# Experts' idle products placed ahead of the ranks, late pieces asked for first, the last group's sums reordered, and attention's samples four abreast

## The chip, the cores and the metric

One core of one Trainium2 chip runs the whole program in one launch. The metric is the time of one execution on the device in microseconds (us); a kernel's figure is the median of its runs.

## The reference

One step of a two-layer decoder in float32, for 256 prompt tokens and 8 samples of 4 new tokens (288 rows of 1024 in all).

```python
h = x + gdn_mixer(rms_norm(x))                    # layer 0: gated DeltaNet
h = h + hier_moe(rms_norm(h), layer 0)            # 32 experts, top 1 group, top 2 in it
k, v = shared_kv(h)                               # rotary keys
h = h + diff_mixer(rms_norm(h), k, v)             # layer 1: differential attention, 8 heads
h = h + hier_moe(rms_norm(h), layer 1)
y = rms_norm(h)

# an expert, d_ff 512:  (silu(x @ w_gate[e]) * (x @ w_up[e])) @ w_down[e]
# differential attention, head of 2 x 64: softmax of each half, a = p[0] - lam * p[1], o = a @ v
# samples attend to 256 cached keys (two pages of 128, from a page table) and their own 4
```

The outputs are the normed rows, the new keys and values, and the DeltaNet and convolution states.

## The kernel before

The program is a sequence of phases with a barrier of all engines after each: `gdn_phase`, `moe_phase` of layer 0, `attn_phase`, `moe_phase` of layer 1, `final_phase`. Each phase gives every engine its own list of work, and semaphores order them. Every float32 product or transpose is two instructions on TensorE.

**Expert layer (`moe_phase`).** The 32 experts are taken two by two in 16 groups (`LAST` is 15). An expert takes up to 64 rows; a pair fills 128 partitions. Weights come in pieces of 2 MB, one matrix of one expert each, six to a group in the order gate, gate, up, up, down, down. They go into ten slots by number (`p % 10`). SP asks for a piece when the products that read its slot have been made (`used`). Pieces 0 to 9 fit in at the start: some are asked for in the phase ahead; in layer 0 4, 5, 7 and 8, in layer 1 4 and 5, at the start of this phase, after the stores of the normed rows (`xn_dram`, which POOL's gathers read); piece 9 only when the stores have landed and group 0's rows have been made. Pieces 10 and 11 wait for group 0's gate products.

The front: TensorE transposes the rows and makes the router's logits; VectorE works out the two experts of each row (`both`, L2105, semaphore `hots`); TensorE counts ranks (L2311 to L2316); VectorE makes a selection matrix for group 0 (`sel0`, L2118); TensorE makes group 0's rows with it (L2411) and the tables for POOL's gathers (L2417), and then the group's gate, up and down products. `keep_busy(n)` issues n products whose result nobody reads (L2306); they keep TensorE at work while it waits. There are 20 ahead of the ranks and 8 behind.

A group in the middle (`gate_up`, `rows_T`, `products`): gate stage (L2334), the transposes of the last group's selection (`sel_T`, L2365), up stage (L2334), the five sums of the group before (`combine`, L2372 and L2375: four of 128x512 and one of the 32 sample rows) with the transposes of the hidden rows between (`hid_T`, L2342), the next group's rows (L2325), the down stage (L2348). A stage is 32 instructions. VectorE adds each sum to the residual rows (`add`, L2222; L2226 for the four parts of the sample rows), forms the hidden product (`hidden`, L2191) and the selection (`selection`). In the last group the sums of group 14 come after the up stage, as elsewhere, and its own five after the down stage, the sample rows' last.

**Attention samples (`attn_phase`, `samples(pair)`).** The 8 samples go in 4 pairs. For a pair TensorE transposes the keys of 2 samples x 2 pages x 8 heads (L1650), VectorE and ACT copy them to `XK`; it makes the scores (L1659), where `QBs` holds the queries of each head in a 64-column block that is zero elsewhere, so that the 8 heads add up into 64 rows a sample, two samples abreast; 12 idle products (L1637) run while VectorE and ACT make the softmax; it combines and transposes the weights (L1664 to L1666), makes the values (L1677) in four 32-column strips, one head each, and transposes the result (L1684), from which VectorE copies each head's own rows (L1520). SP asks for the next pair's keys when a pair's transposes are made and for its values when the value products are; ahead of pair 1's keys it asks for `w_out` (4 MB) and one piece for layer 1.

## Time and profile before

| | |
|---|---|
| median of 3 runs | 1651.73 us (1651.51 to 1653.41) |
| the profiled execution | 1656.28 us, span 1654.5 us |
| mean granted TensorE clock | 0.969 of full speed |
| TensorE busy, its weight loads, VectorE, ScalarE, POOL | 93%, 49%, 40%, 16%, 5% of the span |
| transfers | 485.55 MB, 293 GB/s over the span |
| expert layers, from their first product to their last sum | 365.8 to 857.3 us and 1152.2 to 1641.0 us |
| attention | 858.3 to 1151 us, its sample pairs 969.7 to 1053.6 us |

The span runs from the first to the last instruction; the execution's own time is longer by what lies around it. Busy shares are averages over phases with different limits, and a waiting engine is only of interest where its work is what the phase ends with. "Granted clock" is the share of TensorE's 2.4 GHz that the chip let through.

### The profile page before, as it was taken

The page shows a single profiled execution, that of the slowest core. Times are in us where ns is not written, and L with a number is a line of the kernel's source. Part 1 is how long each engine was busy: PE and PEld are TensorE (multiplying, and loading weights), DVE is VectorE, ACT ScalarE, POOL GpSimd, SP SyncE. Part 2 cuts the span into 40 slices and gives each one's busy share as a digit, 9 for nine tenths or more (in the row PEclk, how much of TensorE's full clock was granted, in tenths as well). Part 3 has the DMA queues.
Part 4 walks back from the last instruction along what each step waited for, and adds up shares of the span by engine and source line. Part 5 has one row for each costly group of instructions (what it writes and reads, how often), then busy time and mean ns, then how long its engine had stood idle before and what let it go on. Part 6 is the DMA issues. An engine that isn't in the chain of part 4 may idle for free. (4 is left out here: it accounts for less than half of the span.)

```text
span 1654.5 us, 21283 instructions
## 1 busy us (share of the span) xinstructions
PE 1541.2 (93%) x8183; PEld 802.8 (49%) x8183; DVE 658.3 (40%) x1654; ACT 268.1 (16%) x653; POOL 82.1 (5%) x139
## 2 busy tenths in 40 slices
PE   9999998998999999989989978869999999998995
PEld 8787776666333333333334445654633333333332
DVE  2756475445324232423252232552532433242424
ACT  2424334220000000000020011451000000000001
POOL 0101010100000000000000000100000000000000
PEclk9999999998999999999989989989899999999998
DMA  6432413438999999999991265603699999999993
GB/s 215 137 107 70 134 43 128 183 131 325 429 429 430 430 430 430 431 431 430 423 352 39 102 258 207 219 5 148 229 429 431 430 430 429 430 431 430 431 420 122
DMA packets 95052, 485.55 MB, mean 293 GB/s; under 512 B 15338, under 2 KB 50062, under 8 KB 70914
## 3 DMA queue, kind: packets, MB, share of 16 engines
q1 hardware_dynamic: 90658, 480.08, 71.6%
q0 software_dynamic: 4320, 4.42, 0.8%
q8 instruction: 54, 0.88, 0.2%
q14 instruction: 20, 0.16, 0.0%
HBM read 484.82 MB, written 10.97 MB: 300 GB/s over the span
## 5 line engine op out<-in xcount | busy, mean ns | idle before, releaser
L2334 PE MATMUL moe_ps_up<-slots,moe_xrT 128*64 128x512 f32 x1024 | 234.8, 612 | 26.4 <-DMA slots<-in_w_up_e_dram 26.4
L2334 PE MATMUL moe_ps_gate<-slots,moe_xrT 128*64 128x512 f32 x1024 | 229.0, 600 | 0.0
L2348 PE MATMUL moe_ps_y<-slots,router_inputs 128*64 128x512 f32 x1024 | 226.8, 595 | 0.0
L2191 DVE TENSOR_TENSOR router_inputs<-router_inputs,moe_ps_up 128x512 f32<-128x512 f32 x32 | 22.0, 688 | 445.4 <-PE moe_ps_up L2334 445.4
L2334 PEld LDWEIGHTS moe_ps_up<-slots,moe_xrT 128*64 128x64 f32 x1024 | 78.5, 141 | 158.2 <-issue 157.5
L2334 PEld LDWEIGHTS moe_ps_gate<-slots,moe_xrT 128*64 128x64 f32 x1024 | 76.1, 138 | 146.9 <-issue 146.8
L2348 PEld LDWEIGHTS moe_ps_y<-slots,router_inputs 128*64 128x64 f32 x1024 | 70.5, 137 | 133.2 <-issue 132.7
L907 PE MATMUL gdn_bank<-gdn_xT,slots 128*128 128x288 f32 x512 | 133.0, 409 | 0.7 <-ACT slots L455 0.7
L907 PEld LDWEIGHTS gdn_bank<-gdn_xT,slots 128*128 128x128 f32 x512 | 93.9, 190 | 24.8 <-issue 1.8
L2012 ACT COPY moe_xrT<-moe_ps_x 128x512 f32<-128x512 f32 x32 | 18.8, 586 | 423.4 <-PE moe_ps_x L2325 393.5
L2372 PE MATMUL moe_ps_x<-moe_y_sb,router_inputs 128*128 128x512 f32 x128 | 63.8, 618 | 0.0
L2214 DVE COPY moe_y_sb<-moe_ps_y 128x512 f32<-128x512 f32 x30 | 20.8, 692 | 91.8 <-PE moe_ps_y L2348 91.8
L1981 POOL DMA_INDIRECT moe_xrT<-xn_rows,moe_rows_in x30 | 30.9, 1030 | 478.6 <-PE moe_ps_x L2325 476.7
L2226 DVE TENSOR_TENSOR resid<-resid,moe_ps_up 32x256 f32<-32x256 f32 x128 | 52.9, 413 | 3.0
L2222 DVE TENSOR_TENSOR resid<-resid,moe_ps_x 128x512 f32<-128x512 f32 x64 | 44.0, 688 | 23.9 <-PE moe_ps_x L2372 23.9
L2017 ACT ACTIVATE router_inputs<-moe_ps_gate 128x512 f32<-128x512 f32 x32 | 19.1, 598 | 206.8 <-PE moe_ps_gate L2334 206.8
L2206 DVE TENSOR_SCALAR moe_place<-consts,moe_lpos,moe_gcur 128x128 f32<-128x128 f32 x192 | 52.1, 345 | 1.2
L2027 ACT COPY moe_y_sb<-moe_ps_y 128x512 f32<-128x512 f32 x32 | 18.8, 586 | 206.5 <-PE moe_ps_y L2348 206.5
L1613 PE MATMUL at_bank<-slots,at_XK 128*128 128x512 f32 x96 | 44.1, 622 | 0.0
L2372 PEld LDWEIGHTS moe_ps_x<-moe_y_sb,router_inputs 128*128 128x128 f32 x128 | 21.7, 189 | 41.3 <-issue 41.3
L1613 PE MATMUL at_pair<-slots,at_XK 128*128 128x512 f32 x96 | 41.5, 592 | 0.0
L665 DVE SCALAR_TENSOR_TENSOR slots<-slots,gdn_cw 128x312 f32<-128x312 f32 x72 | 39.2, 545 | 2.5
(486 smaller groups left out, 1925.8 us busy)
## 6 DMA issues: line engine op xcount, KB each, us to landing
slots<-in_w_gate_e_dram SPq DMA_DIRECT2D x64, 2048.0 KB, 31.2
slots<-in_w_up_e_dram SPq DMA_DIRECT2D x64, 2048.0 KB, 29.7
slots<-in_w_down_e_dram SPq DMA_DIRECT2D x60, 2048.0 KB, 31.3
slots<-in_w_in_a_dram SPq DMA_DIRECT2D x16, 1024.0 KB, 5.6
slots<-in_w_down_e_dram SPq DMA_DIRECT2D x8, 1024.0 KB, 29.8
slots<-in_w_kv_dram SPq DMA_DIRECT2D x4, 2048.0 KB, 17.3
slots<-in_cache_k_dram SPq DMA_DIRECT2D x16, 512.0 KB, 5.0
slots<-in_cache_v_dram SPq DMA_DIRECT2D x16, 512.0 KB, 5.5
```

The costliest lines, as they stand in the source:

```text
L665: ins = V.scalar_tensor_tensor(acc[:, a, j, 0:ACC_COLS], src, cw[:, a, j, tap:tap + 1], acc[:, a, j, 0:ACC_COLS], ALU.mult, ALU.add)
L907: last = T.matmul(PB[i % 2][:, 0:T_ALL], w4[:, j, k, 128 * a:128 * a + 128], xT[:, k, :], start=(k == 0), stop=(k == KT - 1))
L1613: last = T.matmul(bank[:, :], XK[:, 0 if j < 2 else 1, k, at[t]], wslot[3 * half + j][:, k, :], start=(k == 0), stop=(k == KT - 1))
L1981: pool.indirect_dma_start(xg, None, xn_dram[:, :], bass.IndirectOffsetOnAxis(rows_in[:, :], 0), bounds_check=T_ALL - 1, oob_is_err=False). ...
L2191: V.tensor_tensor(hid, hid, ps_up[:], ALU.mult).then_inc(s["hidden"], 1)
L2206: last = V.tensor_scalar(place[:, k, t, :], m["lanes"][:, :], where[:, k, t:t + 1], gcur[:, k, t:t + 1], ALU.is_equal, ALU.mult)
L2214: V.tensor_copy(y_sb[:, 0:512], ps_y[:, 0]).then_inc(s["y0_kept"], 1)
L2222: V.tensor_tensor(half, half, banks[i][:, :], ALU.add).then_inc(s["summed"], 1)
L2226: V.tensor_tensor(part, part, banks[i][32 * q:32 * q + 32, 0:256], ALU.add).then_inc(s["summed"], 1)
L2334: last = T.matmul(ps[64 * e:64 * e + 64, :], xgT[:, k, 64 * e:64 * e + 64], slots[:, slot[2 * n + e], 512 * k:512 * k + 512], start=(k == ...
L2348: last = T.matmul(ps_y[64 * e:64 * e + 64, h, :], hidT[:, k, 64 * e:64 * e + 64], slots[:, slot[4 + e], 1024 * k + 512 * h:1024 * k + 512 ...
L2372: last = T.matmul(banks[i][:, :], selT[:, at[t]], y_sb[:, 512 * h:512 * h + 512], start=True, stop=True)
```

## The change

- The 28 idle products of the expert layer's front: 38 ahead of the ranks, none behind them.
- SP asks for the late pieces at the start of the expert phase, ahead of the rows' stores.
- Last group: group 14's sums come after the gate stage and the selection's transposes, ahead of the up stage; the fifth of them goes to `ps_y`'s first bank. Then up, `sel_T(LAST)`, `hid_T(LAST)`, down. The last group's own sums are six: the two of the left half, the sample rows' two left parts, their two right parts, the two of the right half.
- Attention samples: scores of four heads a strip (two strips a sample, four abreast), the queries in blocks of 32 columns; value products of 512 columns (four heads' values at once) in four strips, 24 instructions a pair for 96; four copies of the result a pair for two. The constants follow the new order of the rows.

In the diff, edits of constants and counts that follow from these are left out.

```diff
-        QBs = sb("QBs", [128, 2, H, 64])
+        QBs = sb("QBs", [128, 2, H, 32])
...
-        QB = flat[1][:, 0:4096].rearrange("p (b h r) -> p b h r", b=DEC_BATCH, h=H)
+        QB = flat[1][:, 0:2048].rearrange("p (b h r) -> p b h r", b=DEC_BATCH, h=H)
...
             for c in range(2):
                 for h in range(H):
-                    V.tensor_copy(QB[64 * c:64 * c + 64, :, h, 32 * c + 4 * h:32 * c + 4 * h + 4],
+                    V.tensor_copy(QB[64 * c:64 * c + 64, :, h, 16 * c + 4 * (h % 4):16 * c + 4 * (h % 4) + 4],
                                   qTd[64 * c:64 * c + 64, h, :].rearrange("p (b q) -> p b q", q=DEC_SEQ)).then_inc(s["QB_made"], 1)
...
                 for b in range(2):
-                    own = (B[3][:, 0:36 * H], B[3][:, 512 - 36 * H:])[b].rearrange("p (h r) -> p h r", h=H)[:, :, (0, 32)[b]:(0, 32)[b] + DEC_SEQ]
-                    V.tensor_copy(oT[:, :, bass.ds(8 * pair + (SEQ + DEC_SEQ * b), DEC_SEQ)], own).then_inc(s["od_kept"], 1)
+                    for f in range(2):
+
+                        base, lo = 64 * b + 48 * f + 12, 16 * (b * f)
+                        own = B[3][:, lo:lo + 496].rearrange("p (j r) -> p j r", j=4)[:, :, base - lo:base - lo + DEC_SEQ]
+                        V.tensor_copy(oT[:, 4 * f:4 * f + 4, bass.ds(8 * pair + (SEQ + DEC_SEQ * b), DEC_SEQ)], own).then_inc(s["od_kept"], 1)
...
-                for h in range(H):
+                for h in range(4):
                     for b in range(2):
-                        last = T.matmul(B[0][64 * b:64 * b + 64, 0:T_ALL], QBs[:, b, h, :], XK[:, b, h, :], start=(h == 0), stop=(h == H - 1))
+                        for f in range(2):
+                            lane = 64 * b + 32 * f
+                            last = T.matmul(B[0][lane:lane + 32, 0:T_ALL], QBs[:, b, 4 * f + h, :], XK[:, b, 4 * f + h, :],
+                                            start=(h == 0), stop=(h == 3), tile_position=(0, lane))
                 last.then_inc(s["S_made"], 1)
 
                 keep_busy(B[1], 256, 12)
@@ -1667,19 +1675,17 @@
                 pe.wait_ge(s["aT_kept"], 2 * pair + 2)
                 pe.wait_ge(s["V0_in"], 64 * pair + 64)
 
-                for b in range(2):
-                    for f in range(2):
-                        for i in range(N_PAGES + 1):
-                            for h in range(4 * f, 4 * f + 4):
-                                values = Vc[:, b, i, 128 * h:128 * h + 128] if i < N_PAGES else v_t[0:T_DEC, 2, 128 * h:128 * h + 128]
-                                weights = aT[:, i, 32 * b:32 * b + 32] if i < N_PAGES else aT[0:T_DEC, 2, 32 * b:32 * b + 32]
-                                lane = 32 * (h % 4)
-                                last = T.matmul(B[2][lane:lane + 32, 256 * b + 128 * f:256 * b + 128 * f + 128], weights, values,
-                                                start=(i == 0), stop=(i == N_PAGES), tile_position=(0, lane))
+                for i in range(N_PAGES + 1):
+                    for b in range(2):
+                        for f in range(2):
+                            lane, e = 64 * b + 32 * f, slice(512 * f, 512 * f + 512)
+                            values = Vc[:, b, i, e] if i < N_PAGES else v_t[0:T_DEC, 2, e]
+                            weights = aT[:, i, 32 * b:32 * b + 32] if i < N_PAGES else aT[0:T_DEC, 2, 32 * b:32 * b + 32]
+                            last = T.matmul(B[2][lane:lane + 32, :], weights, values, start=(i == 0), stop=(i == N_PAGES), tile_position=(0, lane))
                 last.then_inc(s["od_made"], 1)
                 pe.wait_ge(s["rows_kept"], pair + 1)
                 if later(pair):
-                    pe.wait_ge(s["od_kept"], 2 * pair)
+                    pe.wait_ge(s["od_kept"], 4 * pair)
                 for j in range(4):
                     last = T.transpose(B[3][:, 128 * j:128 * j + 128], rot[:, 128 * j:128 * j + 128], ident[:, :])
                 last.then_inc(s["od_T"], 1)
...
         ps_sum = [flat_x[0], flat_x[1], ps_tab, ps_gate, ps_up]
-        ps_sum_last = [flat_x[1], ps_tab, ps_gate, flat_x[0], ps_up]
+        ps_sum_14 = [flat_x[0], flat_x[1], ps_tab, ps_gate, ps_y[:, 0, :]]
+        ps_sum_last = [flat_x[1], ps_tab, ps_gate, flat_hid, flat_x[0], ps_up]
+        LAST_SUMS = [(0, 0), (0, 1), (0, 2), (1, 2), (1, 0), (1, 1)]
...
         @block.sync
         def _(sp):
+            m["prefetch"](sp, layer, (4, 5) if layer else (4, 5, 7, 8))
             for t in range(NT):
                 sp.wait_ge(s["normed"], t + 1)
                 sp.dma_start(xn_dram[128 * t:128 * t + rows[t], :], xn[0:rows[t], t, :]).then_inc(s["xn_stored"], 16)
-            m["prefetch"](sp, layer, (4, 5))
             if layer == 0:
-                m["prefetch"](sp, layer, (7, 8))
                 m["attn_inputs"](sp)
             sp.wait_ge(s["xn_stored"], 16 * NT)
...
+            for i in range(5):
+                add(LAST - 1, i, ps_sum_14)
             selection(LAST, False, lpos, gcol[:, :, :, LAST])
             hidden(LAST)
-            for i in range(3):
-                add(LAST - 1, i, ps_sum)
             turned(LAST)
-            for i in range(3, 5):
-                add(LAST - 1, i, ps_sum)
             dve.wait_ge(s["y_h0"], 1)
             V.tensor_copy(y_sb[:, 0:512], ps_y[:, 0]).then_inc(s["y0_kept"], 1)
-            for i in range(5):
-                add(LAST, i, ps_sum_last)
+            for i in range(6):
+                dve.wait_ge(s["sum_made"], 5 * LAST + i + 1)
+                h, t = LAST_SUMS[i]
+                if t < 2:
+                    half = resid[:, t, 512 * h:512 * h + 512]
+                    V.tensor_tensor(half, half, ps_sum_last[i][:, :], ALU.add).then_inc(s["summed"], 1)
+                else:
+                    for q in range(2 * h, 2 * h + 2):
+                        part = resid[0:T_DEC, 2, 256 * q:256 * q + 256]
+                        V.tensor_tensor(part, part, ps_sum_last[i][32 * q:32 * q + 32, 0:256], ALU.add).then_inc(s["summed"], 1)
...
 
             pe.wait_ge(s["xT_kept"], 2 * NT)
-            keep_busy(20)
+            keep_busy(38)
...
                 T.matmul(ps_count, ones[0:rows[t], :], both[0:rows[t], t, :], start=(t == 0), stop=(t == NT - 1))
-            keep_busy(8)
             xgv = by_tile(xg)
...
             slot, filled = pieces(LAST)
-            gate_up(LAST, slot, filled)
+            pe.wait_ge(s["gx_kept"], 2 * LAST + 2)
+            pe.wait_ge(s["silued"], LAST)
+            pe.wait_ge(s["summed"], 8 * LAST - 12)
+            stage(0, ps_gate, slot, filled)
+            sel_T(LAST - 1, flat_hid)
+            outputs_kept(LAST - 1)
+            for i in range(5):
+                if i == 3:
+                    pe.wait_ge(s["silued"], LAST + 1)
+                combine(LAST - 1, i, ps_sum_14)
+            pe.wait_ge(s["hidden"], LAST)
+            pe.wait_ge(s["summed"], 8 * LAST - 8)
+            stage(1, ps_up, slot, filled)
+            pe.wait_ge(s["summed"], 8 * LAST)
             sel_T(LAST, flat_x[0])
+            hid_T(LAST)
             pe.wait_ge(s["hid_kept"], MAIN_GROUPS)
             for h in range(2):
                 pe.wait_ge(down_half[h], 32)
                 down(slot, h).then_inc((s["y_h0"], s["y_made"])[h], 1)
-            pe.wait_ge(s["summed"], 8 * LAST)
             pe.wait_ge(s["sel_kept"], MAIN_GROUPS)
-            for i in range(5):
-                if i in (0, 2):
-                    pe.wait_ge((s["y0_kept"], s["y1_kept"])[i // 2], MAIN_GROUPS)
-                combine(LAST, i, ps_sum_last)
+            for i in range(6):
+                h, t = LAST_SUMS[i]
+                if i in (0, 3):
+                    pe.wait_ge((s["y0_kept"], s["y1_kept"])[h], MAIN_GROUPS)
+                if t < 2:
+                    last = T.matmul(ps_sum_last[i][:, :], selT[:, at[t]], y_sb[:, 512 * h:512 * h + 512], start=True, stop=True)
+                else:
+                    for q in range(2 * h, 2 * h + 2):
+                        last = T.matmul(ps_sum_last[i][32 * q:32 * q + 32, 0:256], selT[:, at[2]], y_sb[:, 256 * q:256 * q + 256], start=True, stop=True,
+                                        tile_position=(0, 32 * q))
+                last.then_inc(s["sum_made"], 1)
```

## Rows read from the trace of the kernel before

**Rows 1.** Waits inside the expert layers: engine and line waited for whom, us, times, longest.
```profile
PE moe_ps_up L2334 <- DMA slots<-in_w_up_e_dram: 26.4, 14, 2.5
```
**Rows 2.** Windows: length, busy PE, PEld, DVE, ACT, POOL, clock, DMA share, GB/s.
```profile
404.00:408.00 4.00, 4.00 (x22) 1.42 (x20) 3.60 (x23) 0.00 (x0) 0.00 (x0) 1.00 0.45 181
...
412.00:416.00 4.00, 4.00 (x22) 1.60 (x18) 0.59 (x1) 0.00 (x0) 0.00 (x0) 1.00 0.99 426
```
**Rows 3.** Timeline, layer 0's front: start, length, engine, line; in brackets idle time before.
```profile
373.66 4.73 PE L2306 MATMUL moe_ps_gate<-consts 128*128 128x128 f32 x40
...
382.37 0.26 DVE L2105 TENSOR_TENSOR moe_both<-moe_oneh 128x96 f32<-128x96 f32 x1
...
382.68 0.46 PE L2311 MATMUL moe_ps_up<-moe_both,consts 128*128 128x96 f32 x2 [4.29 <-DVE moe_both L2105]
...
384.55 1.07 DVE L2118 TENSOR_SCALAR moe_y_sb<-moe_y_sb,moe_pos 128x64 f32<-128x64 f32 x6
...
385.65 3.78 PE L2306 MATMUL moe_ps_gate<-consts 128*128 128x128 f32 x16
...
389.23 8.71 PE L2411 MATMUL moe_ps_x<-moe_y_sb,moe_last_slot 128*128 128x128 f32 x48
...
399.66 8.78 PE L2334 MATMUL moe_ps_gate<-slots,moe_xrT 128*64 128x512 f32 x32
```
**Rows 4.** Windows of the same front; the third number from the end is the granted clock.
```profile
384.00:386.00 2.00, 2.00 (x9) 1.87 (x9) 1.58 (x9) 0.00 (x0) 0.00 (x0) 0.50 1.05 451
...
400.00:402.00 2.00, 2.00 (x8) 0.61 (x6) 1.76 (x10) 0.00 (x0) 0.89 (x2) 0.52 0.92 307
```
**Rows 5.** Timeline, layer 1's front.
```profile
1160.05 4.73 PE L2306 MATMUL moe_ps_gate<-consts 128*128 128x128 f32 x40
...
1167.50 0.26 DVE L2105 TENSOR_TENSOR moe_both<-moe_oneh 128x96 f32<-128x96 f32 x1
...
1174.43 8.65 PE L2411 MATMUL moe_ps_x<-moe_y_sb,moe_last_slot 128*128 128x128 f32 x48
```
**Rows 6.** Timeline, SP's queue in layer 0's front.
```profile
373.17 4.32 SPq L1904 DMA_DIRECT2D xn_rows<-moe_last_slot  x3
```
**Rows 7.** Timeline, layer 0's last group on TensorE.
```profile
827.72 0.61 PE L2365 MATMUL moe_ps_hid<-consts,moe_place 128*128 128x128 f32 x3
...
830.34 1.97 PE L2334 MATMUL moe_ps_up<-slots,moe_xrT 128*64 128x512 f32 x4 [2.00 <-DMA slots<-in_w_up_e_dram]
...
838.95 1.98 PE L2372 MATMUL moe_ps_x<-moe_y_sb,router_inputs 128*128 128x512 f32 x4
...
844.16 7.09 PE L2348 MATMUL moe_ps_y<-slots,router_inputs 128*64 128x512 f32 x32
```
**Rows 8.** Timeline, layer 1's last group.
```profile
1612.99 0.61 PE L2365 MATMUL moe_ps_hid<-consts,moe_place 128*128 128x128 f32 x3
...
1627.84 6.66 PE L2348 MATMUL moe_ps_y<-slots,router_inputs 128*64 128x512 f32 x30
...
1639.20 1.75 DVE L2226 TENSOR_TENSOR resid<-resid,moe_ps_up 32x256 f32<-32x256 f32 x4
```
**Rows 9.** Timeline, the scores and the values of pair 3.
```profile
1039.40 4.10 PE L1659 MATMUL at_pair<-at_XK,at_QBs 128*64 128x288 f32 x32 [0.75 <-ACT at_XK L1367]
...
1047.90 0.64 PE L1677 MATMUL at_pair<-slots,at_aT 128*32 128x128 f32 x16 [0.50 <-DVE at_aT L1513]
...
1051.73 0.69 DVE L1515 COPY at_rot<-at_pair 128x512 f32<-128x512 f32 x1 [3.89 <-PE at_pair L1677]
```
**Rows 10.** Timeline: three strips abreast with their loads; transposes of pairs 1 and 3.
```profile
955.06 7.07 PE L1621 MATMUL at_pair<-slots,at_XK 128*32 128x512 f32 x48
...
955.51 0.12 PEld L1621 LDWEIGHTS at_pair<-slots,at_XK 128*32 128x32 f32 x3 [0.31 <-issue]
...
994.67 3.29 PE L1650 MATMUL at_bank<-consts,slots 128*128 128x128 f32 x16 [4.38 <-DMA slots<-in_cache_k_dram]
...
1034.05 1.96 PE L1650 MATMUL at_bank<-consts,slots 128*128 128x128 f32 x16
```

More of the change, by code:

```diff
@@ L1176, in attn_constants @@
     c["causal"] = np.concatenate([causal, np.zeros((128, 128)), causal], 1)
-    rb, rc, rh, rq = p // 64, (p // 32) % 2, (p // 4) % 8, p % 4
+    rb, rc, rq = p // 64, (p // 16) % 2, p % 4
+    rh = 4 * ((p // 32) % 2) + (p // 4) % 4
     kb, kq = np.arange(T_DEC) // DEC_SEQ, np.arange(T_DEC) % DEC_SEQ
@@ L1183, in attn_constants @@
     col = np.arange(64)
-    c["halves"] = (rb[:, None] == col // 32) & (rh[:, None] == (col // 4) % 8) & (rq[:, None] == col % 4)
+    ch = 4 * ((col // 16) % 2) + 3 - (col // 4) % 4
+    c["halves"] = (rb[:, None] == col // 32) & (rh[:, None] == ch) & (rq[:, None] == col % 4)
     c["first_half"] = rc[:, None] == 0
@@ L1528, in _ @@
             st["base"], st["n"] = PAIRS * S_STEPS + pre, 0
-            dve.wait_ge(s["od_kept"], 2 * PAIRS)
+            dve.wait_ge(s["od_kept"], 4 * PAIRS)
             V.tensor_tensor(rot2[:, 0:256].rearrange("p (h r) -> p h r", h=H), oT[:, :, SEQ:], oT[:, :, SEQ:], ALU.mult).then_inc(s["od_sq"], 1)
@@ L2214, in kept, with add @@
                 V.tensor_copy(y_sb[:, 0:512], ps_y[:, 0]).then_inc(s["y0_kept"], 1)
-            def add(g, i, banks):
-                dve.wait_ge(s["sum_made"], g * 5 + i + 1)
+            def add(g, i, banks, extra_sum=0):
+                dve.wait_ge(s["sum_made"], g * 5 + (i + 1 + extra_sum))
                 if i < 4:
@@ L2272, in _ @@
                     for i in range(5):
-                        add(g, i, ps_sum)
+                        add(g, i, ps_sum, 1)
                 dve.wait_ge(s["summed"], extra * 8 + 8 * MAIN_GROUPS)
```

## The prediction

> **What bounds the kernel now.** I first read where the expert layers wait, since they fill most of the span. In the list of waits TensorE's one large wait inside them is for the up-projection pieces, some 1.9 us at a time [rows 1]. In the windows the transfers stand nearly still in the last microseconds before group 0's gate products end, and afterwards run at 426 GB/s [rows 2]. The reader should see two regimes: until gate(0) has ended nothing more can be asked for (the slots are full), and from then on the weight stream never stops until the last group's up piece lands. So an expert layer's end is *end of gate(0)* + *a stream of fixed bytes* + *the tail after the last up piece*. TensorE work in the middle is worth nothing; a microsecond before the end of gate(0), or in the tail, is worth a microsecond. Then I read the timeline of the fronts [rows 3, 5] with the granted clock [rows 4], the SP queue [rows 6], the tails [rows 7, 8] and the sample pairs of attention [rows 9], which are a chain without an overlap from pair to pair.
>
> **Front, idle products.** Now 20 idle products (40 instructions) take 4.73 us to 378.4, TensorE then idles to 382.68, and the clock is 0.50 while it does the ranks and the 8 idle products behind them [rows 3, 4]. Those 8 run from 385.65, and the rows' products (L2411) start only at 389.23, although their input, the selection of L2118, is ready at 384.55 + 1.07 = 385.62.
> With 38 in front: 76 instructions x 0.114 us (4.73 less a tail of 0.17, by 40) = 8.7 us, so TensorE is free at 373.66 + 8.7 = 382.3, before L2105 ends at 382.63. Layer 0 loses nothing by it. In layer 1 the free time is 1160.05 + 8.7 = 1168.75 against 1167.76 [rows 5]: 1.0 late. The ranks' eight instructions at half clock take 382.68 to 384.35; I take 1.1 us at full clock (0.6 less). L2118 then ends at about 385.1 (layer 0) and 1171.2 (layer 1), and the counts' six instructions are done before. L2411 starts at 385.2 instead of 389.23, **4.0 us** earlier, and at 1171.25 instead of 1174.43, **3.2 us** earlier.
> What removing the 8 may cost: they are what TensorE does just before the clock comes back. Without them 2.7 us of tiny products and waiting stand before L2411, and a low spell in it is likely, as one follows the idle stretch now, and another the small products ahead of gate(0) [rows 4]. Gate(0) lost 8.78 - 7.09 = 1.7 us to such a spell [rows 3, 7]: the row of the down products shows what 32 such instructions take at the full clock. L2411 loses less, since at full clock it already takes 8.7/48 = 0.18 us per instruction against 0.114 for the idle ones: between 0 and 1.7, I take **1.0 us per layer**. The spell in gate(0) itself I leave as it is; if it goes, 1.7 per layer come on top. Fronts: 3.0 + 2.2 = **5.2 us**. Bounds: 2.6 for the two together (spells at 1.7 each and the ranks no faster) and 7.2 + 3.4 = 10.6 (no spell at all).
>
> **Late pieces ahead of the rows.** SP now holds the rows' stores at 373.17 to 377.5 ahead of the late pieces [rows 6]; the change asks for pieces 4, 5, 7, 8 at about 366 in layer 0. Moved past are three stores of rows, and behind the pieces in layer 0 the five attention inputs, not due for 500 us. 4 x 2.1 MB at 426 GB/s [rows 2] is 19.7 us: the pieces are in by 388 and the stores (1.15 MB) by 391. The stores are late next, and two things wait for them: piece 9 on SP, which must also wait for L2411's end (385.2 + 8.7 + 1.0 = 394.9), and the gather of POOL, which waits for the table, 2 us later still. Both are later than 391: cost nothing, cover 4 us. The gain is a condition, not a term: L2411 ending early would otherwise find the four pieces still in transfer, and piece 9 and the pieces asked for at gate(0)'s end behind them; now the queue is empty by then. In layer 1 two pieces move over an idle queue: nothing.
>
> **Last group.** TensorE now waits 2.00 us for the up piece, then makes up(15), and only then sums group 14 [rows 7]. The change sums group 14 (4.2 us of products: 838.95 to 844.16 less 0.5 each for the hidden product's and the selection's transposes) ahead of up(15).
> Layer 0: gate(15) ends 827.72, transposes 0.6, ACT's copy of the selection until 828.8, sums until 833.05. Up(15) 7.1 us, to 840.1; hidden product 0.7, its transposes 0.5, their copy 0.7, three handovers: down starts at 842.3 instead of 844.16, **1.9 us**. Most of this is that up(15) began after 2 us of idling and took 838.95 - 830.34 = 8.6 us instead of 7.1; that idling goes.
> Layer 1: gate(15) ends 1612.99 [rows 8], so by the same steps sums until 1618.3, up(15) to 1625.4, down at 1627.6 instead of 1627.84, **0.2 us**. The sums that left the way behind up(15) are paid nearly in full by its later start.
> Last sums: VectorE is the limit, four additions of 0.69 and four small ones of 1.75 together, 4.5 us; now it waits a little for each product and has the four small ones last [rows 8]. With small ones in the middle it should wait for nothing after the first: about 0.35 us per layer, **0.7 us**. Tails: **2.8 us**; bounds 0.5 and 4.
>
> **Attention samples.** Scores: 32 instructions two abreast in 4.10 us [rows 9], that is 16 steps of 0.24 and the last one's tail. The same 32, four abreast, are 8 steps: 8 x 0.24 + 0.17 = 2.1, **2.0 less**. That four column strips share a step at full rate is read from three: L1621's 48 instructions of 512 columns take 7.07 us [rows 10], 16 steps of 0.43 (and 0.24/288 per column is the same rate).
> Values: 96 instructions of 128 columns from 1047.90 to about 1051.67, 3.77 us [rows 9]; now 24 of 512. The columns are the same: 24 x 0.107 before and 6 x 0.43 after, both 2.56. Gained is the overhead at the seven changes between full and 32-row operands, of which one stays: 3.77 - (2.56 + 0.13 + 0.17) = **0.9 less**. The Trainium skill (TensorEngine Tiling, Tiling Modes) says that changing the tiling mode drains TensorE; the row agrees.
> Per pair 2.9 us. But pair 1 begins when its keys land: TensorE idles 4.38 us and more before 994.67 [rows 10], and the keys are asked for when pair 0's have been transposed, which the change doesn't move. Pair 0's 2.9 us go into that wait. What pair 1 gains after its keys stays, and the later pairs' transposes wait for no transfer [rows 10]: 3 x 2.9 = 8.7 us. The four small copies of the outputs instead of two cost VectorE 0.3 us each pair, hidden by the next pair's transposes save in the last: 8.7 - 0.3 = **8.4 us**. POOL's copies and clearing halve, off the path. Bounds: 4 (below) and 9.
>
> **Sum.** 5.2 + 2.8 + 8.4 = 16.4 us. The profiled execution took 1656.28 us (span 1654.5); it gives 1639.9. The median of the runs lies 4.55 below that execution, so 1651.73 - 16.4 = **1635.3 us**.
>
> **Rivals.**
> *No low spells in the fronts.* The early, gapless idle products keep the clock through gate(0). For it: the spell now follows an idle stretch that is filled. Against it: the second spell follows small products that stay. 16.4 + 2.0 + 3.4 = 21.8: 1629.9 us.
> *Loads don't hide.* Four strips of the same rows: if a step had to wait for its loads, 0.12 us for the group [rows 10], the scores would take 8 x 0.36 + 0.17 = 3.05 and the values 6 x 0.55 + 0.3 = 3.6, per pair 1.2 less instead of 2.9, and the sum is 11.3: 1640.4 us. L1621's steps show no such addition with three strips. The Trainium skill (TensorE: Matmul & The Clock Gate, Part 3: Packing small matmuls) states this rule, that weight loads overlap running products only where the row groups differ; the trace speaks against it.
> *The fronts give nothing.* TensorE at half clock from the ranks through L2411 eats the 4.0 and 3.2, or the stores come so late that piece 9 holds up the stream: 11.2 left, 1640.5 us.
> *Slower.* One mechanism: with fewer instructions under way the clock falls in the sample pairs. Price: pair 1's first 16 transposes took 3.29 us at the low clock [rows 10]; the same 16 in pair 3, at the full clock, took 1.96. Applied to all TensorE work of a pair (about 11 us of 16) it is some +11 per pair, +34 for three, and the total +17: 1669 us. It decides from half of the pairs' time on. Against it: the change halves one stretch of 4.1 us, and the 12 idle products stay.
> *It does nothing*: the stream would have to be set by something other than gate(0)'s end, and attention by transfers.
>
> **How the numbers follow.** Forecast 0.62, no spells 0.18, loads 0.06, fronts nothing 0.09, slower 0.03, nothing 0.02. The range goes from the no-spells case with a little of the bounds, 1628, to the two weaker ones, 1641.5. What can be told from no change is about 0.2%, 3.3 us: all cases but the last two are faster by more. Faster 0.95, same 0.02, slower 0.03.
>
> **What would show it.** After: no idling between idle products and ranks; L2411 about 2.6 us (layer 0) and 3.5 us (layer 1) behind L2105's end instead of 6.6 and 6.7; the score products about 2.1 us per pair, the value products 2.9; the wait for pair 1's keys longer by 2.9; up(15) in both layers starting without a wait for its piece and some 2.7 us after it lands; last VectorE additions of 512 columns. The stream must still be unbroken from gate(0) on. It would be wrong if the clock is at 0.50 through all of L2411 and gate(0), if the scores take over 3 us, or if the rows' stores land after L2411 ends.

## The result, and the profile after

| | before | after |
|---|---|---|
| median of 12 runs | 1657.64 us (1651.51 to 1660.91) | 1645.63 us (1641.24 to 1649.47) |
| the profiled execution | 1656.28 us, span 1654.5 us | 1645.96 us, span 1644.2 us |
| mean granted TensorE clock | 0.969 | 0.968 |

The ratio of after to before is **0.9932, 95% interval [0.9916, 0.9948]**: faster by 11.3 us (8.6 to 13.9) where the sum said 16.4. Two things stand between 1635.3 and 1645.63, and they are kept apart below. The median of before rose from 1651.73 to 1657.64 us with nine more runs: 5.9 us of the miss is the base that the sum was taken from. The other 4.4 us (5.1 by the ratio) are terms of the sum.

I cut both spans at the same events. In us, before and then after:

| stretch | before | after | change | forecast |
|---|---|---|---|---|
| start to layer 0's experts | 365.8 | 366.5 | +0.7 | |
| layer 0: front, to the start of up(0) | 42.5 | 45.6 | **+3.1** | -3.0 |
| layer 0: up(0) to the end of gate(15) | 419.5 | 419.4 | 0 | 0 |
| layer 0: tail, to attention's first product | 30.6 | 28.5 | -2.1 | -2.2 |
| attention | 293.9 | 282.5 | -11.3 | -8.4 |
| of it the four sample pairs | 84.4 | 76.4 | -8.0 | -8.4 |
| layer 1: front | 41.3 | 37.6 | -3.6 | -2.2 |
| layer 1: up(0) to the end of gate(15) | 419.6 | 422.7 | +3.2 | 0 |
| layer 1: tail, to the last sum | 28.0 | 27.5 | -0.5 | -0.55 |
| final phase | 13.6 | 13.8 | +0.3 | |

The rows sum to -10.3, the difference of the spans, 6.1 us short of the forecast. Layer 0's front is 6.1 off and layer 1's expert stream 3.2; the first and the last row add 1.0; attention (2.9) and layer 1's front (1.4) came out better than forecast. So one front went the wrong way, and it weighs as much as the whole miss. Timeline of layer 0's front after the change:

```profile
374.38 8.75 PE L2319 MATMUL moe_ps_gate<-consts 128*128 128x128 f32 x76
...
383.07 0.26 DVE L2112 TENSOR_TENSOR moe_both<-moe_oneh 128x96 f32<-128x96 f32 x1
...
383.38 0.46 PE L2324 MATMUL moe_ps_up<-moe_both,consts 128*128 128x96 f32 x2 [0.25 <-DVE moe_both L2112]
...
384.70 1.07 DVE L2125 TENSOR_SCALAR moe_y_sb<-moe_y_sb,moe_pos 128x64 f32<-128x64 f32 x6
...
385.82 14.25 PE L2423 MATMUL moe_ps_x<-moe_y_sb,moe_last_slot 128*128 128x128 f32 x48 [0.58 <-DVE moe_y_sb L2125]
400.00 3.18 PE L2429 MATMUL moe_ps_tab<-moe_entry,moe_place 128*128 128x32 f32 x12
...
403.11 9.15 PE L2346 MATMUL moe_ps_gate<-slots,moe_xrT 128*64 128x512 f32 x32
```

Up to 385.82 it goes as forecast: the idle products fill the wait, the ranks start 0.3 us behind L2112 (the old L2105), and the selection is ready at 385.77. Then the same 48 instructions that took 8.71 us [rows 3] take 14.25. Windows of that stretch (the third number from the end is the granted clock, the next the DMA share):

```profile
384.00:386.00 2.00, 1.42 (x12) 1.27 (x12) 1.77 (x12) 0.00 (x0) 0.00 (x0) 1.00 1.01 426
386.00:388.00 2.00, 2.00 (x10) 1.56 (x10) 1.90 (x8) 0.00 (x0) 0.00 (x0) 0.70 1.07 295
388.00:390.00 2.00, 2.00 (x8) 1.52 (x7) 1.44 (x10) 0.00 (x0) 0.00 (x0) 0.50 0.79 242
...
396.00:398.00 2.00, 2.00 (x8) 1.45 (x7) 0.00 (x0) 0.00 (x0) 0.00 (x0) 0.50 0.00 0
...
404.00:406.00 2.00, 2.00 (x8) 0.71 (x6) 1.78 (x8) 0.00 (x0) 1.20 (x1) 0.50 0.97 418
406.00:408.00 2.00, 2.00 (x8) 0.52 (x6) 1.73 (x10) 0.00 (x0) 0.00 (x0) 0.68 0.60 232
408.00:410.00 2.00, 2.00 (x12) 0.62 (x10) 1.97 (x14) 0.00 (x0) 0.27 (x1) 1.00 0.03 8
```

The clock is full through the ranks, at its lower level (0.50) from about 387 to 407.3, and full again from 408: one low spell of 20 us, where before there were two shorter ones [rows 4] with the rows' products at full clock between them. TensorE is busy all the while. Before, the clock was back just as the rows' products had begun behind the eight idle ones, as these windows of that kernel show:

```profile
388.00:390.00 2.00, 2.00 (x11) 1.95 (x10) 1.28 (x9) 0.00 (x0) 0.00 (x0) 0.54 0.98 418
390.00:392.00 2.00, 2.00 (x14) 1.57 (x12) 0.00 (x0) 0.00 (x0) 0.00 (x0) 1.00 0.99 426
```

After the change the DMA share is near nothing from 394 on, so the late pieces and the rows' stores have landed, 3 us later than estimated and still 6 before L2423 ends. Layer 1's front, with the same code, has no such spell; its timeline:

```profile
1150.39 8.75 PE L2319 MATMUL moe_ps_gate<-consts 128*128 128x128 f32 x76
1158.97 0.36 PE L2324 MATMUL moe_ps_up<-moe_both,consts 128*128 128x96 f32 x2
...
1161.31 8.51 PE L2423 MATMUL moe_ps_x<-moe_y_sb,moe_last_slot 128*128 128x128 f32 x48 [0.58 <-DVE moe_y_sb L2125]
1171.54 8.78 PE L2346 MATMUL moe_ps_gate<-slots,moe_xrT 128*64 128x512 f32 x32
```

and the window of its rows' products, with the clock at 1.00:

```profile
1161.00:1170.00 9.00, 8.69 (x51) 6.76 (x51) 3.86 (x21) 0.14 (x1) 0.00 (x0) 1.00 0.01 2
```

Attention's samples, timeline of TensorE from pair 1's keys to pair 2's, against [rows 9, 10]:

```profile
994.96 3.32 PE L1655 MATMUL at_bank<-consts,slots 128*128 128x128 f32 x16 [6.97 <-DMA slots<-in_cache_k_dram]
...
1001.68 2.15 PE L1666 MATMUL at_pair<-at_XK,at_QBs 128*32 128x288 f32 x32 [0.75 <-ACT at_XK L1369]
...
1008.25 1.92 PE L1684 MATMUL at_pair<-slots,at_aT 128*32 128x512 f32 x16 [0.50 <-DVE at_aT L1515]
1010.10 1.06 PE L1684 MATMUL at_pair<-at_v,at_aT 32*32 32x512 f32 x8
...
1012.66 1.96 PE L1655 MATMUL at_bank<-consts,slots 128*128 128x128 f32 x16
```

The scores are the 2.1 us of the forecast, the values 2.91 (1008.25 to 1011.16) against 2.9. The wait for pair 1's keys grew from 4.38 to 6.97 us: pair 0's gain went in there.

Layer 0's last group, and the end of layer 1's sums on VectorE, against [rows 7, 8]:

```profile
832.67 1.96 PE L2384 MATMUL moe_ps_x<-moe_y_sb,router_inputs 128*128 128x512 f32 x4 [0.58 <-ACT router_inputs L2029]
...
836.84 7.09 PE L2346 MATMUL moe_ps_up<-slots,moe_xrT 128*64 128x512 f32 x32
...
844.72 0.74 PE L2354 MATMUL moe_ps_hid<-consts,router_inputs 128*128 128x128 f32 x4 [0.24 <-DVE router_inputs L2198]
846.25 7.09 PE L2360 MATMUL moe_ps_y<-slots,router_inputs 128*64 128x512 f32 x32 [0.78 <-DVE router_inputs L2203]
```

```profile
1627.30 0.84 DVE L2273 TENSOR_TENSOR resid<-resid,moe_ps_gate 32x256 f32<-32x256 f32 x2
1628.18 0.87 DVE L2273 TENSOR_TENSOR resid<-resid,moe_ps_hid 32x256 f32<-32x256 f32 x2
1629.08 0.69 DVE L2269 TENSOR_TENSOR resid<-resid,moe_ps_x 128x512 f32<-128x512 f32 x1
1629.68 0.68 DVE L2269 TENSOR_TENSOR resid<-resid,moe_ps_up 128x512 f32<-128x512 f32 x1
```

Up(15) follows the sums without a wait, and the additions run without gaps.

### The profile page after: what moved, and what is told of

The parts are those of the page before. It is cut to its first block and busy times, and to the rows that moved or that the text cites. A ratio compares the mean times of both kernels' runs of the same rounds, so it can differ in the third digit from the quotient of the medians.

```text
span 1644.2 us, 20799 instructions
## 1 busy us (share of the span) xinstructions
PE 1535.7 (93%) x7935; PEld 793.2 (48%) x7935; DVE 658.9 (40%) x1662; ACT 268.1 (16%) x653; POOL 79.1 (5%) x139
## 5 line engine op out<-in xcount | busy, mean ns | idle before, releaser
L2346 PEld LDWEIGHTS moe_ps_gate<-slots,moe_xrT 128*64 128x64 f32 x1024 | 76.2, 139 | 149.0 <-issue 148.9
L2384 PE MATMUL moe_ps_x<-moe_y_sb,router_inputs 128*128 128x512 f32 x120 | 59.5, 618 | 1.2 <-ACT router_inputs L2029 1.2
L2229 DVE TENSOR_TENSOR resid<-resid,moe_ps_x 128x512 f32<-128x512 f32 x60 | 41.3, 688 | 32.0 <-PE moe_ps_x L2384 32.0
L2233 DVE TENSOR_TENSOR resid<-resid,moe_ps_up 32x256 f32<-32x256 f32 x112 | 46.3, 413 | 2.6
```

What stands on the lines that cost most here:

```text
L2229: V.tensor_tensor(half, half, banks[i][:, :], ALU.add).then_inc(s["summed"], 1)
L2233: V.tensor_tensor(part, part, banks[i][32 * q:32 * q + 32, 0:256], ALU.add).then_inc(s["summed"], 1)
L2346: last = T.matmul(ps[64 * e:64 * e + 64, :], xgT[:, k, 64 * e:64 * e + 64], slots[:, slot[2 * n + e], 512 * k:512 * k + 512], start=(k == ...
L2384: last = T.matmul(banks[i][:, :], selT[:, at[t]], y_sb[:, 512 * h:512 * h + 512], start=True, stop=True)
```

## The experiments

### One part alone

Three kernels: before with attention's edits, with the fronts' (idle products, late pieces), with the tails'.

> The kernel before with the attention samples four abreast and nothing else of the change. By the terms measured in the changed kernel's trace (scores 2.15 us a pair for 4.10, values 2.96 for 3.84, pairs 16.3 us apart for 19.0) pairs 1 to 3 give 8.1 us; the forecast said 8.4. If the profiled difference of the whole attention phase (294 us to 282.5, 11.3 us) is due to the edit, it is 11 us. If the rest of it is only where TensorE's low clock spells fell, about 8 us in the median. Fronts and tails as before: the rows' products (L2411 of before) start 6.6 us behind the end of the VectorE line that makes both.

> The kernel before with 38 idle products ahead of the ranks, none behind, and the late pieces asked for ahead of the rows' stores; attention and tails as before. Theory A (clock): without the idle products behind the ranks the clock can fall in front of the rows' products and, since these are thin, does not come back until the gate stage: in a layer where it falls they take about 14 us instead of 8.6 and the front ends 3 to 4 us later than before, in a layer where it doesn't the front is 3.5 us shorter. The median lies between -7 and +7 us, near 0, and the executions spread over 7 us. Theory B (transfers): the front is slow because the pieces of 2 MB and the rows' stores are now in transfer under the rows' products; then both layers, or always layer 0, show it, whatever the clock. My forecast of before said -5.2 us.

> The kernel before with only the last group's order changed. Forecast 2.8 us less (2.2 in layer 0, 0.6 in layer 1), which the changed kernel's trace bears out for layer 0 (2.1). If a low clock spell in up(15) of layer 0 was most of that gain and falls elsewhere in other executions, about 1 us.

| | median us | ratio [interval] | in us of 1656 | forecast |
|---|---|---|---|---|
| attention only | 1646.65 | 0.9939 [0.9917, 0.9961] | -10.1 | -8.4 |
| fronts only | 1655.34 | 0.9985 [0.9968, 1.0001] | -2.5 | -5.2 |
| tails only | 1655.33 | 0.9993 [0.9977, 1.0009] | -1.2 | -2.8 |

Attention carries nearly the whole change; its interval, 6.5 to 13.6 us, takes in both the 8 and the 11 us of the expectation. That of the fronts takes in nothing and, at its edge, the forecast 5.2. With the fronts alone the spell is there too, so neither the tails nor attention make it. Its timeline, the rows' products of layers 0 and 1:

```profile
385.94 14.25 PE L2409 MATMUL moe_ps_x<-moe_y_sb,moe_last_slot 128*128 128x128 f32 x48 [0.58 <-DVE moe_y_sb L2117]
...
1178.94 8.51 PE L2409 MATMUL moe_ps_x<-moe_y_sb,moe_last_slot 128*128 128x128 f32 x48 [0.58 <-DVE moe_y_sb L2117]
```

The tails' interval takes in both nothing and the 2.8 us; the profile has to decide there, and shows up(15) and the sums as in the whole change.

### Is it the clock or the transfers?

Two theories for layer 0's front: the clock falls since nothing dense stands between the ranks and the rows' products, or the stores and pieces asked for together hold something up. First, the changed kernel with eight idle products back behind the counts:

```diff
                 T.matmul(ps_count, ones[0:rows[t], :], both[0:rows[t], t, :], start=(t == 0), stop=(t == NT - 1))
+            keep_busy(8)
```

> The changed kernel with the 8 idle products put back behind the ranks (38 in front, 8 behind). Theory A: the clock stays up through the rows' products in both layers, which take 8.6 us each; they start later by what the 8 cost at full clock beyond the wait for the selection, 16 x 0.114 = 1.8 less the 0.6 of waiting now there = 1.2 us. Layer 0's front ends 4 us earlier than in the changed kernel's profile, layer 1's 1.2 us later; the median of the kernel is lower than the changed kernel's by 0 to 3 us and its runs lie closer together. Theory B (transfers): the rows' products in layer 0 take 14 us again and everything is 1.2 us later in both layers.

1639.61 us, ratio 0.9892 [0.9869, 0.9915]. Its timeline, layer 0:

```profile
385.66 2.05 PE L2319 MATMUL moe_ps_gate<-consts 128*128 128x128 f32 x16
387.55 8.41 PE L2424 MATMUL moe_ps_x<-moe_y_sb,moe_last_slot 128*128 128x128 f32 x48
...
397.80 8.60 PE L2347 MATMUL moe_ps_gate<-slots,moe_xrT 128*64 128x512 f32 x32
```

Windows of it, with the clock at 1.00 where the changed kernel had 0.70 and 0.50:

```profile
386.00:388.00 2.00, 2.00 (x20) 1.96 (x18) 1.86 (x9) 0.00 (x0) 0.00 (x0) 1.00 1.09 344
388.00:390.00 2.00, 2.00 (x14) 1.55 (x12) 1.86 (x12) 0.00 (x0) 0.00 (x0) 1.00 0.88 211
```

Counted from the ranks, the eight delay the rows' products by 1.2 us; they shorten them by 5.8. Layer 0's front takes 39.3 us instead of 45.6. Layer 1's, where there was no spell to take away, takes 40.3 instead of 37.6: the 1.2 us of delay, and 1.5 us more in the table's products and gate(0) (2.54 and 9.64 us instead of 1.86 and 8.78). The profiles' fronts thus give 3.6 us together; the ratios differ by 6.6 us, with some 4.6 of uncertainty, where the expectation had 0 to 3. Then the other side, the changed kernel with the late pieces asked for behind the rows' stores, as before:

```diff
-            m["prefetch"](sp, layer, (4, 5) if layer else (4, 5, 7, 8))
             for t in range(NT):
...
+            m["prefetch"](sp, layer, (4, 5))
             if layer == 0:
+                m["prefetch"](sp, layer, (7, 8))
```

> The changed kernel with the late pieces asked for after the rows' stores, as before. Theory B (transfers under the rows' products slow them, or the stores behind the pieces hold something up): layer 0's rows' products are back at about 8.6 us. Theory A: they take 14 us as in the changed kernel, and as they end so late (400 us) the pieces are in either way: the ratio to the kernel before is that of the changed kernel, 0.993.

1646.38 us, 0.9934 [0.9908, 0.9960], against 0.9932 of the changed kernel, and the rows' products of layer 0 take 14.45 us. The order of the requests is not the cause, and it is worth nothing where the rows' products end as late as here; whether it is where they end early, at 392, no run shows. In another form, five idle products in the counts' place and the counts behind the rows' products:

```diff
-            for t in range(NT):
-                T.matmul(ps_count, ones[0:rows[t], :], both[0:rows[t], t, :], start=(t == 0), stop=(t == NT - 1))
+            keep_busy(5)
...
             last.then_inc(s["gx_T"], 1)
+            for t in range(NT):
+                T.matmul(ps_count, ones[0:rows[t], :], both[0:rows[t], t, :], start=(t == 0), stop=(t == NT - 1))
```

> The changed kernel, but the counts' six thin instructions come behind the rows' products and 5 idle products (10 instructions, 1.14 us) stand in their place, where TensorE waits for the selection. If it is the thin stretch between the ranks and the rows' products that lets the clock fall (theory A), the clock stays up in layer 0 as well, with no delay to the rows' products: 8.5 us in both layers and 5.5 us less than the changed kernel in the profile of layer 0. If a stretch as short as the four rank products and what is left of the wait still lets it fall, layer 0 shows about 14 us again. Layer 1 the same as in the changed kernel but for 0.9 us of counts, which come before the tables.

1641.38 us, 0.9907 [0.9884, 0.9930]; rows' products 8.51 us in both layers, and again layer 1's front is 2.5 us longer than the changed kernel's. The theory of the transfers fell, that of the clock stands: the two kernels that put idle products right ahead of layer 0's rows' products make them in 8.4 to 8.5 us. The four with the same order of the products and no idle ones right ahead (the changed kernel, the fronts alone, the one with the requests as before, and the one with late output weights further down) take 14.25, 14.25, 14.45 and 13.33, wherever the requests stand. By the windows the clock falls in these four only about 0.8 to 2.2 us after the rows' products have begun. What makes it fall is therefore not shown, only that either idle products ahead or another order of the products themselves (the next experiment) keeps the long spell away. Why layer 1, where the same work went by at full clock each time, is spared is open: what differs in the rows is that its ranks follow the idle products at once, while layer 0's wait 0.25 us for L2112, and no run here separates the two.

### Rows' products that are dense themselves

The loop goes tile by tile within a column block: 128 rows, 128 rows, 32 rows, eight times. Here the full-height tiles of all blocks come first and the 32-row tile's products last:

```diff
-            for k in range(KT):
-                for t in range(NT):
-                    last = T.matmul(ps_x[:, k // 4, k % 4, :], by_tile(xn[0:rows[t], t, :])[:, k, :], sel0[0:rows[t], t, :],
-                                    start=(t == 0), stop=(t == NT - 1))
+            for part in ((0, 1), (2,)):
+                for k in range(KT):
+                    for t in part:
+                        last = T.matmul(ps_x[:, k // 4, k % 4, :], by_tile(xn[0:rows[t], t, :])[:, k, :], sel0[0:rows[t], t, :],
+                                        start=(t == 0 and k % 4 == 0), stop=(t == NT - 1 and k % 4 == 3))
```

> The changed kernel with the rows' products of group 0 in another order: the 32 products of the two full tiles first, the 16 instructions of the 32-row tile after them, in place of a change between 128 and 32 rows at every sixth instruction. If the thinness of these products comes from those changes, as I read 0.178 us an instruction against 0.114 for the idle ones, they take 48 x 0.11 + 0.3 = 5.6 us instead of 8.5 at the full clock. Theory A (clock): they are then dense enough to bring the clock back where it has fallen: layer 0 no longer shows 14.25 us but 7 to 8, with one short low spell, and the low stretch that ran on into the gate stage is gone. Fronts 6 to 9 us (layer 0) and 3 us (layer 1) shorter than in the changed kernel's profile. Theory B (transfers): no more than 3 us in each. Against the kernel before: ratio 0.985 by A, 0.990 by B.

**1634.19 us, 0.9863 [0.9834, 0.9891].** Its timeline, both fronts:

```profile
386.06 5.82 PE L2424 MATMUL moe_ps_x<-moe_y_sb,moe_last_slot 128*128 128x128 f32 x48 [0.58 <-DVE moe_y_sb L2125]
393.59 8.79 PE L2346 MATMUL moe_ps_gate<-slots,moe_xrT 128*64 128x512 f32 x32
402.21 7.04 PE L2346 MATMUL moe_ps_up<-slots,moe_xrT 128*64 128x512 f32 x32
...
1154.96 5.82 PE L2424 MATMUL moe_ps_x<-moe_y_sb,moe_last_slot 128*128 128x128 f32 x48 [0.58 <-DVE moe_y_sb L2125]
```

The same instructions but for their order and their start flags: 14.25 to 5.82 us in layer 0 and 8.51 to 5.82 in layer 1. In layer 1 the clock was full in both, so the 2.7 us come from the order: of fifteen changes between 128-row and 32-row operands one is left, an estimate of 0.19 us for each of the fourteen. The Trainium skill (TensorEngine Tiling (Array Packing), Tiling Modes) says that a change of the tiling mode drains TensorE; the trace agrees as far as the changes cost time, but shows no drain as such. The rest of layer 0's gain, 5.7 us, is the clock.

With the idle products in the counts' place too:

> Both of the last two edits: fronts at the full clock with rows' products of 5.6 us. By theory A about 3 us a layer under the kernel with 8 idle products behind the ranks (which measured a ratio of 0.989), and no wait of 1.2 us for them: ratio 0.984 to 0.987. By theory B no better than that kernel.

1635.43 us, 0.9871 [0.9847, 0.9895]; 5.82 us in both layers, up(0) at 403.74. By the ratio no different from the tiles' order alone; in the profiles each front is some 2.5 us longer (38.0 and 37.3 us for 35.5 and 34.9), as the counts stand behind the rows' products and the tables and gate(0) run longer at the lower clock.

Then the order in the kernel before, where the eight idle products still stand (the edit is the same):

> The kernel before with nothing but the new order in the rows' products (tiles 0 and 1 of all column blocks first, the 32-row tile's products behind them). Theory (two separate costs): with the 8 idle products in place the clock is full there already, so what the order saves is only the changes between 128-row and 32-row operands, 8.7 to 5.8 us, 2.9 us in each layer; both end the stretch ahead of gate(0), so the total falls by 5.8 us, ratio 0.9965. Rival: the order helps only by bringing the clock back, which the kernel before doesn't need: then the rows' products stay at 8.5 us or the gain goes into the next wait, and the ratio is 1.000.

**This expectation missed.** 1655.06 us, ratio 1.0001 [0.9986, 1.0017]: nothing, where I had 5.8 us. The products did get shorter, by 2.3 and 2.9 us:

```profile
390.12 6.41 PE L2412 MATMUL moe_ps_x<-moe_y_sb,moe_last_slot 128*128 128x128 f32 x48
...
398.26 8.78 PE L2334 MATMUL moe_ps_gate<-slots,moe_xrT 128*64 128x512 f32 x32
...
1166.58 5.71 PE L2412 MATMUL moe_ps_x<-moe_y_sb,moe_last_slot 128*128 128x128 f32 x48
...
1174.59 9.79 PE L2334 MATMUL moe_ps_gate<-slots,moe_xrT 128*64 128x512 f32 x32
```

In layer 0 the front is 2.7 us shorter than before (39.8 us for 42.5), in layer 1 it is not (41.0 for 41.2): the clock was at 0.50 over that layer's start, its idle products take 5.87 us instead of 4.73, and gate(0) 9.79 instead of 8.78. The window of that start:

```profile
1142.00:1160.00 18.00, 16.74 (x87) 16.01 (x88) 12.30 (x27) 4.81 (x8) 1.62 (x2) 0.53 0.37 134
```

The profile of before has no such spell there. It is one execution, at 1648.87 us the shortest of the twelve, so it doesn't explain the median. To see all runs I took span x (1 - clock) of each, half the time at the lower clock, and means over the runs:

| kernel (runs) | mean span | clock | span x (1 - clock) |
|---|---|---|---|
| before, runs beside this one (17) | 1653.8 | 0.9671 | 54.4 us |
| before, full tiles first (12) | 1653.1 | 0.9654 | 57.2 us |
| changed (12) | 1643.6 | 0.9691 | 50.8 us |
| changed, full tiles first (6) | 1632.4 | 0.9723 | 45.2 us |

Read as what the clock cost, the order saves 3.5 us at full clock on the kernel before and loses 2.8 more to the clock; on the changed kernel it saves on both counts. This is a rough estimate. The 2.8 us have a standard error of some 1.6, and the split counts low time in which TensorE only waits as well. For the tails alone the same working gives 3.8 us more at full clock and 5.0 less to the clock, of an edit that hardly changes TensorE's work. Why the shorter products don't show in the time of the kernel before stays open.

### What delayed pair 1's keys

SP asks for `w_out` and one piece, 6.3 MB, ahead of them, and neither is needed before the end of attention. Moved behind pair 3's values:

```diff
-            sp.dma_start(w_out, m["w_out_b"][0].rearrange("(h p) n -> p h n", p=128)).then_inc(s["wout_in"], 16)
-            m["prefetch"](sp, 1, (3,))
             with sp.Fori(1, PAIRS) as pair:
                 cache(0, pair, True)
                 cache(1, pair, True)
+            sp.dma_start(w_out, m["w_out_b"][0].rearrange("(h p) n -> p h n", p=128)).then_inc(s["wout_in"], 16)
+            m["prefetch"](sp, 1, (3,))
```

> The changed kernel with one move on SP's queue: the output weights w_out (4.2 MB) and layer 1's piece 3 (2.1 MB), asked for ahead of pair 1's keys, are asked for behind pair 3's values. Theory (my account of the attention part): what pair 0 gained from the narrower products went into the wait for pair 1's keys, and that wait exists only because 6.3 MB are in front of the keys; then pair 1's transposes start as pair 2's do, as soon as pair 0's result is transposed, at 988 instead of 994.96 us: 7.0 us, and up to 1.4 us more as the 16 transposes behind the wait take 1.96 instead of 3.32 us at the full clock. The total falls by 7 to 8.4 us against the changed kernel. Rival: the keys are late for another reason (they are asked for only when pair 0's are transposed, and their own 2.1 MB take that long), or the wait moves on to pair 1's values; then the time stays within 2 us of the changed kernel's. The fronts aren't touched: the rows' products of layer 0 take 14.2 us as in the changed kernel.

> Both amendments together: the rows' products with the full-height tiles first, and w_out with piece 3 behind pair 3's values. They touch different phases, so both theories expect the sum: the 10 us that the order of the tiles gave, and 7 to 8.4 us where the output weights were what delayed pair 1's keys (a time near 1627 us, ratio to the kernel before near 0.981), or nothing more than the first where they weren't (near 1635 us, 0.986).

The first: 1635.70 us, 0.9869 [0.9851, 0.9887]; 10.4 us (0.63 points) below the changed kernel's ratio, with some 4 us of uncertainty, where 7 to 8.4 were expected. Its timeline, pairs 1 and 2:

```profile
987.09 1.91 PE L1655 MATMUL at_bank<-consts,slots 128*128 128x128 f32 x16
...
1003.38 1.85 PE L1655 MATMUL at_bank<-consts,slots 128*128 128x128 f32 x15
```

The wait is gone, the 16 transposes take 1.91 us instead of 3.32, and the four pairs take 69.6 us instead of 76.4. The two together: **1624.88 us, 0.9812 [0.9789, 0.9835]**, 1.3% below the changed kernel's median of 1645.63. The gains of the two add up: 6.9 and 6.3 points in a thousand by themselves, 12.0 together. Its profile shows that the full tiles first don't always keep the clock. Timeline and windows of its layer 0:

```profile
385.29 7.44 PE L2424 MATMUL moe_ps_x<-moe_y_sb,moe_last_slot 128*128 128x128 f32 x48 [0.58 <-DVE moe_y_sb L2125]
```

```profile
386.00:388.00 2.00, 2.00 (x12) 2.00 (x11) 1.93 (x11) 0.00 (x0) 0.00 (x0) 0.50 0.97 221
388.00:390.00 2.00, 2.00 (x14) 2.00 (x14) 0.90 (x7) 0.00 (x0) 0.00 (x0) 0.68 0.81 309
390.00:392.00 2.00, 2.00 (x18) 1.88 (x18) 0.00 (x0) 0.00 (x0) 0.00 (x0) 1.00 1.00 387
```

The clock falls as in the changed kernel, but it is back at about 389.3, within the same products, and not at 407.3: the spell costs 1.6 us.

At last that kernel with the eight idle products back behind the counts, `keep_busy(8)` as above:

> The kernel with the full-height tiles first and the output weights late, with 8 idle products put back behind the counts. In the run without them the rows' products took 7.44 us in layer 0 and 5.82 in layer 1, and gate(0) 7.09 and 8.43. Theory (dense products hold the clock by themselves): the 8 only delay the rows' products, by about 1.5 us in each layer, and give back at most the 1.6 us of layer 0: the time is within 3 us of the kernel without them, on the slow side of it. Rival: gate(0) and the rows' products still lose to the clock, and the idle products win it back: 3 us or more faster than without them.

1624.90 us, 0.9805 [0.9782, 0.9828]: the same. Counted from the ranks, the rows' products start 1.2 us later. In layer 0 they take 5.71 instead of 7.44 us, but gate(0) 8.76 instead of 7.09; in layer 1 gate(0) takes 7.09 instead of 8.43. With the full tiles first, idle products buy back what they cost and no more.

## Why the prediction was wrong, step by step

- **The bound.** Right for layer 0: from the start of up(0) its stream took 419.5 us before and 419.4 after, and 419.2 to 420.0 in every other profile but that with only the output weights late (421.1), so a front's gain or loss reaches the end. For layer 1 it is not borne out: its stream took 3.2 us more after the change, where the sum had nothing, and 421.3 to 423.5 in every kernel but before and before with full tiles first (419.6 and 419.7). In the profile after, a gate piece was 1.7 us late there, and up(14) took 8.78 us for 7.09. The profiles of the parts alone have that slow up stage too, whichever part they hold, and of them attention's has the late piece; what moves it was not tested.
- **Idle products in front.** The schedule was right: TensorE waits 0.25 us for L2112 ahead of the ranks, and the selection is ready at 385.8 in layer 0.
- **"L2411 loses less ... I take 1.0 us per layer."** This step failed. The bound of 1.7 supposed a spell as long as the one in gate(0); this one lasted until gate(0) was half done. In layer 0 the rows' products lost 5.5 us (14.25 for 8.71), the table's products behind them 1.3 (3.18 for 1.86) and gate(0) 0.4 more. The term was 3.0 gained and measured 3.1 lost. In layer 1 they lost nothing (8.51), so 3.6 were gained where the sum had 2.2. Idle products put back ahead of them take the loss away, the full tiles first take all or most of it; the late pieces' place doesn't. What makes the clock fall in layer 0 and not in layer 1 stays open.
- **The rival "the fronts give nothing"** had this mechanism, half clock through L2411, at 0.09. It came true in layer 0 alone; with -0.5 us for both fronts in the profiles it is the case nearest to what happened. The row that should have given it more weight stood in [rows 4]: the clock was at 0.50 while TensorE was busy with small products, and in the windows of before it is at 1.00 only from 390 on, behind the eight idle ones.
- **Late pieces ahead of the rows.** No gain was counted, and none came. The cover was thinner than worked out, landing at 394 instead of 391.
- **Last group.** Layer 0: down starts 1.67 us nearer to gate(15)'s end (1.9 forecast), layer 1 0.08 (0.2), the last sums 0.4 in each (0.35). Together 2.6 us for 2.8. What was short is a wait of 0.58 us for ACT's copy of the selection and one of 0.78 for the copy of the hidden rows.
- **Attention.** Right in mechanism and size: 8.0 us over the four pairs for 8.4, with pair 0's share going into the wait for the keys. The rival that loads don't hide (3.05 us for the scores) fell with 2.15. The Trainium skill (TensorE: Matmul & The Clock Gate, Part 3: Packing small matmuls) states that loads overlap running products only where the row groups differ; here the 32 loads of a pair's scores, 1.62 us of them, lie within the 2.15 us of the products on the same rows, so by this trace the rule does not hold. The other 3.3 us of attention's 11.3 are in its parts ahead of and behind the pairs, whose products the change doesn't touch. In the four profiles with the old samples these parts take 203.2 to 210.5 us (209.4 in before, 206.1 after the change), so the 3.3 can't be told from that scatter and are not claimed for the edit. The pairs themselves scatter too: 84.4 to 87.4 us in those four, 76.2 to 80.7 in the seven with the new samples and the weights asked for as before; the means are 7.2 apart.
- **The base.** 1651.73 us was the median of three runs; the median of twelve is 1657.64, above even the profiled execution's 1656.28. The text took 4.55 us off for the distance between the two, which the further runs don't bear out. Applied to 1657.64, the forecast is 1641.2; measured, 1645.63.

## What to carry to other kernels

Idle products that look spent may be what brings the clock back, or keeps it, for the small products behind them: before they are moved, price a low spell over everything up to the next large products, not over one stage. Products that alternate between full and short operands can be ordered so that all of one height come together; it saves the changes, and here it kept the clock up or had it back within 4 us. A chain that starts with a transfer pays for whatever was asked for ahead of it: ask for the large pieces that are due last behind the small ones that are due next.

## What was not expected of the hardware

- The same 48 float32 products took 5.82 or 8.51 us at full clock, by their order, and 14.25 in the old order at the lower one.
- TensorE had work without a gap from 386 to 408 us, first the rows' products (16 of the 48 instructions on 32 rows), then the table's, and was granted 0.50 of its clock nearly all that time; layer 1's same products ran at 1.00.
- Shorter products in the kernel before left the time where it was (ratio 1.0001), with a mean clock of 0.9654 for 0.9671; why is open.
